# Sums of squares moved into the last jobs of a stage, and two jobs that share each row of h

## The reference

```
def rms_norm(x, g):
    xf = x.astype(F32)
    y = xf * lax.rsqrt(jnp.mean(xf * xf, axis=-1, keepdims=True) + EPS)
    return (y * g.astype(F32)).astype(x.dtype)
...
h = rms_norm(x, p['norm1'][i]) * (1 + sc1) + sh1
...
x = x + gt1 * y.astype(x.dtype)
h = rms_norm(x, p['norm2'][i]) * (1 + sc2) + sh2
f = conv_ffn(h, rows, cols, ...)
x = x + gt2 * f.astype(x.dtype)
```

## Time and profile before

| | us |
|---|---|
| median of 3 runs | 3362.69 (3360.27 to 3363.6) |
| the profiled execution | 3364.44 |
| its span, first to last instruction | 3362.6 |
| granted TensorE clock over the span | 0.967 of full speed |

### The profile page before, as it was taken

One profiled execution on the slowest core, in us unless ns is written; L12 is line 12 of the kernel. 1 busy time (PEld: TensorE's weight loads), 2 busy tenths in 40 slices (PEclk: granted clock), 3 DMA queues, 4 the chain that ended last, 5 costly groups with the idle time before them and its releaser, 6 DMA issues.

```text
span 3362.6 us, 54509 instructions
## 1 busy us (share of the span) xinstructions
PE 3128.3 (93%) x22776; PEld 2952.1 (88%) x22776; DVE 1860.4 (55%) x3390; ACT 1146.1 (34%) x2097; POOL 912.9 (27%) x708
## 2 busy tenths in 40 slices
PE   6899999979999789999997999789999997999998
PEld 5699998969999779999996888679999995999997
DVE  1476374436666536727554454437737543784863
ACT  2333232234444323323223555423323223332322
POOL 0133323322322123233332112123332330333332
PEclk9999999989999799999998999899999998999999
DMA  8133333211111013333312111113333221222121
GB/s 342 72 138 127 135 122 132 72 57 54 51 54 57 30 51 128 134 131 128 101 62 67 48 48 48 46 51 135 127 138 117 96 71 62 66 75 77 54 74 62
DMA packets 95718, 305.78 MB, mean 91 GB/s; under 512 B 11248, under 2 KB 19696, under 8 KB 94832
## 3 DMA queue, kind: packets, MB, share of 16 engines
q1 hardware_dynamic: 85104, 286.71, 24.3%
q10 hardware_dynamic: 10368, 15.57, 1.3%
HBM read 297.52 MB, written 4.72 MB: 90 GB/s over the span
## 4 chain that ended last, share of the span: by engine, by line
PE 88%; DVE 8%; ACT 2%; issue 1%; DMA 1%; ACTq 0%; SPq 0%; DVEq 0%
PE acc L471 57%; PE acc L489 13%; PE acc L453 3%; PE acc L501 3%; PE acc L544 2%; PE acc L675 2%; PE acc L557 2%; PE acc L765 2%; PE acc L534 1%; DVE ffn_sq L1322 1%; DVE h_lo L1336 1%; DVE ffn_acc_v L1724 1%; DVE ffn_rstd L1310 1%; DVE ffn_acc_a L1724 1%; PE acc L597 1%
## 5 line engine op out<-in xcount | busy, mean ns | idle before, releaser
L445 POOL TENSOR_TENSOR w_lo<-w_raw,w_hi 128x512 fp32r<-128x512 f32 x704 | 912.7, 1318 | 2412.5 <-ACT w_hi L879 2412.4
L471 PE MATMUL acc<-h_hi,w_hi 128*128 128x320 f32 x2816 | 888.0, 315 | 39.7 <-DVE h_lo L1336 39.6
L471 PE MATMUL acc<-h_lo,w_hi 128*128 128x320 f32 x2816 | 874.9, 311 | 0.0
L471 PE MATMUL acc<-h_hi,w_lo 128*128 128x320 f32 x2816 | 874.7, 311 | 0.0
L879 ACT ACTIVATE w_hi<-w_raw 128x512 fp32r<-128x512 f32 x704 | 398.6, 611 | 724.6 <-DMA w_raw<-in_wall 394.2
L1724 DVE SCALAR_TENSOR_TENSOR ffn_acc_v<-acc,ffn_conv,ffn_acc_v 128x441 f32<-128x441 f32 (+3 forms) x880 | 544.3, 619 | 104.3 <-ACT ffn_acc_v L1247 104.3
L471 PEld LDWEIGHTS acc<-h_hi,w_hi 128*128 128x128 f32 x2816 | 532.9, 189 | 49.2 <-issue 35.0
L1724 DVE SCALAR_TENSOR_TENSOR ffn_acc_a<-acc,ffn_conv,ffn_acc_a 128x441 f32<-128x441 f32 (+3 forms) x880 | 545.2, 619 | 49.0 <-ACT ffn_acc_a L1247 39.5
L471 PE MATMUL acc<-g_hi,w_hi 128*128 128x320 f32 x1664 | 525.4, 316 | 18.1 <-DVE ffn_acc_a L1724 13.7
L471 PEld LDWEIGHTS acc<-h_lo,w_hi 128*128 128x128 f32 x2816 | 533.5, 189 | 0.0
L471 PEld LDWEIGHTS acc<-h_hi,w_lo 128*128 128x128 f32 x2816 | 532.9, 189 | 0.0
(11 more groups left out here) (174 smaller groups left out, 3300.1 us busy)
## 6 DMA issues: line engine op xcount, KB each, us to landing
w_raw<-in_wall SPq DMA_DIRECT2D x288, 512.0 KB, 4.0
mod_late<-in_wall SPq DMA_DIRECT2D x152, 512.0 KB, 3.3
mod_early<-in_wall SPq DMA_DIRECT2D x40, 512.0 KB, 8.7
w_raw<-in_wall SPq DMA_DIRECT2D x64, 256.0 KB, 2.9
w_raw<-in_wall SPq DMA_DIRECT2D x32, 384.0 KB, 3.0
box<-box_in ACTq DMA_DIRECT2D x2, 3008.0 KB, 16.0
x<-in_x SPq DMA_DIRECT2D x1, 2560.0 KB, 17.8
out_y<-pool_h SPq DMA_DIRECT2D x8, 320.0 KB, 3.0
```

What stands on the lines that cost most here:

```text
L445: nc.gpsimd.tensor_tensor(w_lo[j][:, cols], w_raw[j][:, cols], w_hi[j][:, cols].bitcast(F32), ALU.subtract).then_inc(lo_done, 1)
L471: mm = nc.tensor.matmul(result[j][:, c0:c1], w, h, start=(k == 0 and u == 0), stop=(k == nk - 1 and u == 2), skip_group_check=True)
```

## The change

For norms 2, 3, 4, 5, 6 and 8 (`TAIL_NORMS`) the squares are made by ScalarE among the last eight jobs of the stage before, one row behind the jobs. VectorE adds up the squares of rows 0 to 5 in `sq_sum` (which lies in `hf[0]`), five additions a norm, each after a row of `x` is updated. TensorE then multiplies three times by the constants (the sum, row 6, row 7) where it did so eight times, with no wait for the update of the whole of `x`. The last eight jobs use the slots 1 to 3, so that slot 0 is free for the sum. At the start of the six stages that begin with a split h (four up stages, `hgrn_in`, `diff_in`) the first two jobs run together: each row of h, when released, is multiplied for job 0 (slot 0) and job 1 (slot 1). In up stages the weight units of both jobs come before them. ScalarE copies job 1 of the two mixers out of slot 1.

```
+def result_slot(n):
+    return n % SLOTS if n not in TAIL_AT else 1 + TAIL_AT[n] % 3
+def used_before(n):
+    return n - (SLOTS - 1) if n not in TAIL_AT else n - 2
...
+        ADDED = KT - 3
+        squares_used = [sum(3 if m in TAIL_NORMS else KT for m in range(k)) for k in range(2 * DEPTH + 2)]
+        sq_sum = hf[0]
...
# TensorE
+            def first_pair(n, h_at):
+                for k in range(KT):
+                    for j in (0, 1):
+                        if k in (0, SPLIT):
+                            pe.wait_ge(lo_done, SPLIT_BEFORE[n + j] + k // SPLIT + 1)
+                        if j == 0:
+                            pe.wait_ge(h_ready, h_at + k + 1)
+                        wk = slice(k * P, (k + 1) * P)
+                        hi, lo = w_hi[(n + j) % SLOTS][:, wk], w_lo[(n + j) % SLOTS][:, wk]
+                        for c0, c1 in HALVES:
+                            for u, (w, h) in enumerate(((hi, h_hi), (hi, h_lo), (lo, h_hi))):
+                                mm = nc.tensor.matmul(result[j][:, c0:c1], w, h[:, k, c0:c1], start=(k == 0 and u == 0),
+                                                      stop=(k == KT - 1 and u == 2), skip_group_check=True)
+                        if k == KT - 1:
+                            mm.then_inc(job_done, 1)
...
+            def tail(k, n, nk, hi, lo):
+                for o in range(KT):
+                    job(n + o, nk, hi, lo)
+                pe.wait_ge(sq_added, ADDED * (TAIL_NORMS.index(k) + 1))
+                for c0, c1 in HALVES:
+                    mm = nc.tensor.matmul(result[0][:, c0:c1], ones_h[:], sq_sum[:, c0:c1], start=True, stop=False,
+                                          skip_group_check=True)
+                mm.then_inc(sq_used, 1)
+                for kt in (KT - 2, KT - 1):
+                    sum_row(k, kt)
...
-                    steps(5 * KT)
+                    steps(3 * KT)
...
                             ffn_mod(m)
-                            job(m, KT, lambda k: h_hi[:, k, :], lambda k: h_lo[:, k, :],
-                                KT * split_norms[2 * layer + 1] if m == first["up", layer] else None)
+                            if p0 == 0 and m == n + 1:
+                                first_pair(n, KT * split_norms[2 * layer + 1])
+                            elif p0 or m > n:
+                                job(m, KT, lambda k: h_hi[:, k, :], lambda k: h_lo[:, k, :])
...
# ScalarE
+            def square_row(k, kt):
...
+                    act.wait_ge(updated, before + kt + 1)
...
+                if kt >= 2 and k in TAIL_NORMS:
+                    act.wait_ge(sq_added, ADDED * TAIL_NORMS.index(k) + max(kt - 2, 1))
...
+                nc.scalar.activation(sq[kt % 2][:], x[:, kt, :], ACT.Square).then_inc(sq_done, 1)
+
+            def tail(k, n, a):
+                for o in range(a, KT):
+                    ahead(n + o)
+                    if o:
+                        square_row(k, o - 1)
+                square_row(k, KT - 1)
...
-                    for o in range(1, KT):
-                        ahead(first[("hgrn_out", layer)] + o)
+                    tail(2 * layer + 1, first[("hgrn_out", layer)], 1)
...
# VectorE
+            def add_squares(k, kt):
+                done = ADDED * TAIL_NORMS.index(k) + kt
+                dve.wait_ge(sq_done, KT * k + kt + 1)
+                if kt > 1:
+                    dve.wait_ge(sq_added, done - 1)
+                V.tensor_tensor(sq_sum[:], sq[0][:] if kt == 1 else sq_sum[:], sq[kt % 2][:], ALU.add).then_inc(sq_added, 1)
...
                 for o in range(KT):
                     dve.wait_ge(job_done, n + o + 1)
-                    add_x(o, result[(n + o) % SLOTS], mod[:, layer % 2, :], 2 * (16 + o)).then_inc(job_used, 1)
+                    add_x(o, result[result_slot(n + o)], mod[:, layer % 2, :], 2 * (16 + o)).then_inc(job_used, 1)
+                    if 1 < o < KT - 1:
+                        add_squares(2 * layer + 1, o - 1)
```

More of the change, by code:

```diff
@@ L358, in trunk @@
         N_CONST = 5
+        TAIL_NORMS = [k for k in range(1, 2 * DEPTH + 1) if k % 2 == 0 or k not in (2 * layer + 1 for layer in POOL_LAYERS)]
+        ADDED = KT - 3
+        squares_used = [sum(3 if m in TAIL_NORMS else KT for m in range(k)) for k in range(2 * DEPTH + 2)]
+        sq_sum = hf[0]
         def x_updates(k):
@@ L725, in _ @@
                     pe.wait_ge(o_ready, hd)
-                    n0 = first[("hgrn_out", layer)]
-                    for o in range(KT):
-                        job(n0 + o, KT, lambda k: g_hi[:, k, :], lambda k: g_lo[:, k, :])
+                    tail(2 * layer + 1, first[("hgrn_out", layer)], KT, lambda k: g_hi[:, k, :], lambda k: g_lo[:, k, :])
                 else:
@@ L839, in _ @@
                     pe.wait_ge(o_ready, hd)
-                    n0 = first[("diff_out", layer)]
-                    for o in range(KT):
-                        job(n0 + o, KT, lambda k: g_hi[:, k, :], lambda k: g_lo[:, k, :])
-                norm(2 * layer + 1, first[("up", layer)])
+                    tail(2 * layer + 1, first[("diff_out", layer)], KT, lambda k: g_hi[:, k, :], lambda k: g_lo[:, k, :])
+                if kind == 0:
+                    norm(2 * layer + 1, first[("up", layer)])
                 g_at = NPAIR * layer
@@ L940, in norm @@
+            def tail(k, n, a):
[4 more added lines that the diff above has]
+                square_row(k, KT - 1)
+            def norm(k, plain):
+                if k == 0 or k % 2 and KINDS[k // 2] == 0:
+                    for kt in range(KT):
+                        square_row(k, kt)
+                act.wait_ge(sq_used, squares_used[k + 1])
                 if k % 2 == 0 and 0 < k < 2 * DEPTH:
@@ L1140, in take @@
                         dst = (q2[h % 2], k2[h % 2], dv_t)[part]
-                        nc.scalar.activation(dst[:], result[0], ACT.Copy, scale=SCALE if part == 0 else 1.0).then_inc(job_used, 1)
+                        nc.scalar.activation(dst[:], result[1 if h == 0 and part == 1 else 0], ACT.Copy, scale=SCALE if part == 0 else 1.0).then_inc(job_used, 1)
                     def values(h):
@@ L1219, in _ @@
                     hd += HEADS
-                    for o in range(KT):
-                        ahead(first[("diff_out", layer)] + o)
+                    tail(2 * layer + 1, first[("diff_out", layer)], 0)
                 norm(2 * layer + 1, False)
```

97 lines of the change are left out of this document (55 added, 42 removed).

## The result

The changed kernel takes 3282.74 us (median of 4 runs, 3281.63 to 3285.94), the kernel before 3362.66 beside it (4 runs, 3360.27 to 3363.6): a ratio of 0.9764, 95% interval 0.9749 to 0.9778. That is 79.9 us less, where 76.8 was forecast. The span of the profiled execution is 3280.9 us, that of before 3362.6.

A forecast was written before the change was run, and what follows sets the result against it. TensorE, busy 93% of the span, was taken as the bound, with time to win from its gaps or work taken off it. Gains 40.7 + 23.5 + 4.7 + 7.9 = 76.8 us, from 3362.7 to 3286 us, range 3272 to 3300.

The forecast's parts named there:

- The term of 6.8 us: At each of six norms, the sum of squares behind the last job ends after 3.42 us instead of 10.20; 40.7 us together.
- the upper row of 1.92 us: VectorE's added squares in the last jobs, with GpSimd working: 2.9 us with the add to x, inside a 3.52 us job.
- the second stretch: Low-clock matmuls in job 0 of layer 1's up stage, waiting for rows of h; claimed to go, layer 1 gaining 6.7 us.
- VectorE's taps: Convolution work in up stages, 12.4 us a pair against 14.1 us or more of jobs; layer 3 could lose 1 us.
- the 23.5 us forecast: Up stages' gain from running the first two jobs together: 5.5 in layers 0 and 2, 6.7 in layer 1, 5.8 in layer 3.
- 30.2 and 31.42 us: Time from reciprocal to job 2 before the change, in layer 2's and layer 1's up stages, against 24.7 us forecast.
- Rival C: First pairs stay at 1.2 GHz throughout, ending 33.1 us after the reciprocal; 17 of 41 us lost, 3339 us; chance 0.04.
- 4.7: Recurrence's start: job 2 at 713.7 instead of 718.43, behind a copy, a conversion, a table load and the sigmoid; gain 4.7 us.
- A: Last jobs of the three short stages: late weight loads hold up the squares, +10 us, 3296 us; chance 0.05.
- E: Whole change: the parts do not act, since TensorE waits elsewhere as long; 3363 us; chance 0.02.
- B: Stage starts: the pair gains nothing because copies, convolution or weight units hold job 2; 3322 us; chance 0.05.
- D: First pairs at the low clock, which goes on for two more jobs in each of six stages; 3408 us; chance 0.02.

The follow-up runs named there:

- Experiment 1: The changed kernel with the pair undone, so only the squares among the last jobs remain: 3323.3 us, ratio 0.9881 to the kernel before.
- experiment 3: The changed kernel without VectorE's additions, TensorE multiplying every row of squares itself, five of them among the jobs: 3316.0 us, ratio 0.9861 to the kernel before.
- experiment 4: The changed kernel with a second two-input VectorE instruction, its result unread, before every addition of squares: 3286.4 us, ratio 0.9771 to the kernel before.
- experiment 5: The changed kernel with ScalarE copying jobs 0 and 1 of both mixers before conversions, Sigmoid table first in the recurrence: 3282.5 us, ratio 0.9755 to the kernel before.
- experiment 9: The changed kernel with copies and Sigmoid table first in the recurrence alone, the attention keeping its order: 3281.1 us, ratio 0.975 to the kernel before.
- experiment 2: The changed kernel with the squares' part undone, so only the shared rows of h in the first two jobs remain: 3330.8 us, ratio 0.99 to the kernel before.

## Why the prediction was right

**The norms.** Right, by the step it named: five rows fewer, and the sum 3.25 us long instead of 9.13, with no wait for the add to x before it. The term of 6.8 us was 0.2 too small, as the fp32 instructions are 0.27 us apart in the last rows; the prediction had that as one of its bounds (1 us). Experiment 1 shows the gain without the pair, experiment 3 that most of it comes from the rows that VectorE took.

**VectorE's addition.** The prediction took the upper row of 1.92 us against 0.81; 26 of the 30 take 1.82 or 1.83, the other four 0.82, three of them in the last norm, where GpSimd rests by then. By the page "SBUF — State Buffer" of the Trainium skill (section "Who interferes with whom") the prediction estimated that the fifth addition could make the last add to x 0.6 us late. The trace agrees that the two engines slow each other (the addition 1.83 us instead of 0.82, two halves of w_lo 3.14 instead of 2.55), but not with the estimate: that add starts on time, with 0.77 us idle before it. Only with two such instructions per job (experiment 4) is it late, by 1.3 us.

**The pair.** Right in its mechanism and nearly in every size: a backlog and no idle time behind the first row, a stretch at the low level kept (5 us in four stages), the second stretch gone, 23.8 us to the last matmul. VectorE's taps, the prediction's worry for layer 3, held nothing: the 40 jobs behind job 2 end at the same distances from it as before in all four up stages, and the 1.1 us by which layer 3's stage is longer come later, at waits behind which the clock fell. That the four gains sum to just the 23.5 us forecast is partly luck: layer 0's 6.3 contains a shorter stretch at the low level (2.8 us in this profile; in the second profile of the same kernel it was 4.7, and job 2 started 0.85 later, a gain of 5.4). Over all the profiles with a pair that is not kept busy, that stretch lasts 2.8 to 6.0 us. The prediction's 30.2 and 31.42 us are taken from rows of the chain that begin 0.14 us behind job 2's first matmul. Rival C, with the page "TensorE: Matmul & The Clock Gate" (section "A second HAM failure mode: psum-queue depth-cycling") beside it, is out: matmuls that alternate between two slots rose to 0.147 us in all six stages and stayed there.

**The recurrence.** The order of the copy, the conversion, the table and the sigmoid was right, and so was the gain to job 2's start (4.5 for 4.7). What failed is the silence about what follows: TensorE is idle for 3.1 us there by its timeline, the clock falls, and job 2 takes 9.92 us, 2.6 us more than a job at full clock. The prediction had counted the clock's price behind a norm and not behind this new gap. Experiments 5 and 9 take most of the gap away and get these 2.6 us back. The price is not the same in each execution: in the six profiles that keep the gap (3.1 us each) job 2 takes from 7.29 us to 10.06, the latter in the second profile of the changed kernel; in the four with the copies first it takes 7.29 in all. The lowest, in experiment 4's chain, behind the same gap:

```profile
702.35 7.29 PE acc L525 x48
```

**The stretches in between.** Costed at nothing, they gave 4.1 us in this pair of profiles. 2.8 are in layer 2, where the kernel before had the longer of experiment 9's two lengths and the changed one the shorter. The kernels of experiments 1 and 2, which each hold half of the change, have the longer one, and the changed kernel the shorter in both its profiles: whether these 2.8 us are the change's doing is not shown. Another 3.8 us are at the end of the recurrence, where before TensorE's clock was low behind the same waits (0.61 in the 15 us from 1150 on, 0.89 in those that answer to them after); 2.6 of them make up for the slow job 2. TensorE's timeline there, before:

```profile
1150.27 2.50 PE L675 MATMUL acc<-hgrn_qq,ffn_rstd 128*128 128x128 f32 x10 [1.88 <-DVE hgrn_qq L1500]
1155.70 3.78 PE L706 MATMUL acc<-hgrn_v_tok,hgrn_kt 128*128 128x128 f32 x16 [0.79 <-ACT hgrn_kt L1070]
```

and after:

```profile
1135.02 1.38 PE L729 MATMUL acc<-hgrn_qq,ffn_rstd 128*128 128x128 f32 x10 [1.87 <-DVE hgrn_qq L1584]
1138.69 2.05 PE L760 MATMUL acc<-hgrn_v_tok,hgrn_kt 128*128 128x128 f32 x16 [1.20 <-ACT hgrn_kt L1144]
```

So the change's own steps, norms and pairs, make 77.9 of the 81.9 us between the reciprocals of norms 1 and 8, the slow job takes 2.6 back, and the rest lies mostly where the clock fell or did not. The 3.8 us are there, in whole or in part, in all the other kernels profiled too, one part alone included, against a single profile of the kernel before: whether they are the change's or that profile's stays open. Rivals A and E find nothing in the traces: no square is late, and both parts act alone. Of B the mixers show the part that the forecast had priced: there the copies hold job 2 by 3.1 and 3.3 us, while in the up stages it follows the pair. Of D one job shows, job 2 of the recurrence.

## What to carry to other kernels

Work that stands alone at the end of a stage is worth moving only to an engine that has room there: on TensorE itself, among its jobs, the same sums cost their full time. Where inputs arrive one by one, let two jobs use each; then look at what the second job was hiding, since a gap of TensorE that a change uncovers can be paid twice, as idle time and as work at the low clock behind it. The recurrence's 3.1 us were, in most profiles; the attention's 3.3, with two matmuls in the middle, were not: its job 2 ran at 0.147 us a matmul in both profiles of the changed kernel. A difference of 2 to 3 us in a stage that no edit touches is compared with a second profile of the same kernel before it is explained.

## What was not expected of the hardware

**Two VectorE instructions beside GpSimd.** With one addition in a job it takes 1.83 us. With a product ahead of it, in the three short stages, one of the two takes 1.8 to 1.9 us and the other 0.8 to 1.0 in 12 of 15 jobs, and both are stretched in 3; in the jobs of 7 us before norms 3 and 5 both are, in 9 of 10. GpSimd pays as well, as its timelines at the end of layer 0 show. The kernel before:

```profile
672.29 2.55 POOL L445 TENSOR_TENSOR w_lo<-w_raw,w_hi 128x512 fp32r<-128x512 f32 x2 [0.97 <-ACT w_hi L879]
```

The changed kernel, where the same two halves take 3.14 us:

```profile
666.49 3.14 POOL L468 TENSOR_TENSOR w_lo<-w_raw,w_hi 128x512 fp32r<-128x512 f32 x2 [0.37 <-ACT w_hi L935]
```

**The clock behind equal waits.** The same 3.8, 2.1 and 2.0 us of waiting leave a granted clock of 0.83 and 1.00 or of 0.74 and 0.91 in windows of 20 us. And a pair whose TensorE was kept busy through the norm never fell to the low level, which is worth 1.1 or 1.2 us in each of layers 1 to 3 and not the whole 2.3 that the stretch costs: then there is no backlog, and the last rows of h set the pair's end.

**The start.** The time to norm 1's reciprocal, before any of the changed places, lies between 124.7 and 135.4 us over the profiles, whatever the kernel, so totals of single executions scatter by more than a small part of this change is worth.
